# Strassen's scheme for six of eleven tile pairs of the down products in a one-core decoder layer

## The reference, cut to what matters

```python
def swiglu(x, wg, wu, wd):
    return (jax.nn.silu(x @ wg) * (x @ wu)) @ wd      # 1024 -> 2816 -> 1024

def trunk_layer(...):
    x = layer_norm(DN_ALPHA * x + 0.5 * swiglu(x, wg_l[0], wu_l[0], wd_l[0]), g_l[0], b_l[0])
    y, ks, vs, cs = token_mixer(x, attend, conv_prev, w_in_l, conv_w_l, w_out_l)
    x = layer_norm(DN_ALPHA * x + y, g_l[1], b_l[1])
    x = layer_norm(DN_ALPHA * x + 0.5 * swiglu(x, wg_l[1], wu_l[1], wd_l[1]), g_l[2], b_l[2])
```

## Time and profile before

| | |
|---|---|
| median of 3 runs | 1014.18 us |
| time of the profiled execution | 1012.97 us |
| its span | 1011.2 us |
| PE busy | 981.6 us, 97% of the span |
| DVE busy | 666.4 us, 66% |
| ACT busy | 468.9 us, 46% |
| POOL busy | 118.5 us, 12% |
| mean granted TensorE clock | 0.994 |

### The profile page before, as it was taken

One profiled execution on the slowest core, in us unless ns is written; L12 is line 12 of the kernel. 1 busy time (PEld: TensorE's weight loads), 2 busy tenths in 40 slices (PEclk: granted clock), 3 DMA queues, 4 the chain that ended last, 5 costly groups with the idle time before them and its releaser, 6 DMA issues.

```text
span 1011.2 us, 18213 instructions
## 1 busy us (share of the span) xinstructions
PE 981.6 (97%) x7538; PEld 961.5 (95%) x7538; DVE 666.4 (66%) x964; ACT 468.9 (46%) x780; POOL 118.5 (12%) x120
## 2 busy tenths in 40 slices
PE   7999999999999999999999998999999999999994
PEld 7999999999999999999898998999999999999994
DVE  5797642567776468736667678998534577774466
ACT  4465421255555235555555456664422345553230
POOL 2100000101100000107242012010000000000004
PEclk9999999999999999999999999999999999999998
DMA  9546356445435234362022457063453444445403
GB/s 262 128 114 168 105 114 154 96 121 118 106 95 188 94 116 84 102 193 83 13 74 71 139 155 187 21 168 95 135 147 64 104 105 112 126 140 172 136 1 89
DMA packets 142474, 118.68 MB, mean 117 GB/s; under 512 B 13778, under 2 KB 140470, under 8 KB 142376
## 3 DMA queue, kind: packets, MB, share of 16 engines
q1 hardware_dynamic: 130368, 105.46, 34.8%
q0 software_dynamic: 10880, 10.49, 7.5%
q10 hardware_dynamic: 1144, 1.57, 1.3%
HBM read 113.56 MB, written 4.95 MB: 117 GB/s over the span
## 4 chain that ended last, share of the span: by engine, by line
PE 88%; DVE 6%; ACT 3%; issue 1%; DMA 1%; DVEq 0%; SPq 0%; POOL 0%; ACTq 0%
PE banks L1058 41%; PE banks L1071 24%; PE banks L881 17%; PE banks L1243 2%; DVE w_lo L1821 1%; ACT w_hi L1367 1%; ACT x_hi L1549 1%; DMA w_raw<-in_ffn_w_gate 1%; PE banks L1289 1%; PE banks L1287 1%; DVE rstd L2077 1%; PE banks L935 1%; DVE x_res L2084 1%; DVE x_res L2064 0%; DVE w_lo L1849 0%
## 5 line engine op out<-in xcount | busy, mean ns | idle before, releaser
L1071 PE MATMUL banks<-h_hi,w_hi 128*128 128x280 f32 (+1 forms) x480 | 139.1, 290 | 0.0
L1071 PE MATMUL banks<-h_hi,w_lo 128*128 128x280 f32 (+1 forms) x480 | 139.0, 290 | 0.0
L1071 PE MATMUL banks<-h_lo,w_hi 128*128 128x280 f32 (+1 forms) x480 | 138.8, 289 | 0.0
L881 PE MATMUL banks<-x_hi,w_hi 128*128 128x280 f32 (+1 forms) x416 | 126.2, 303 | 3.9 <-DVE w_lo L1821 1.7
L881 PE MATMUL banks<-x_hi,w_lo 128*128 128x280 f32 (+1 forms) x416 | 120.9, 291 | 0.0
L881 PE MATMUL banks<-x_lo,w_hi 128*128 128x280 f32 (+1 forms) x416 | 120.8, 290 | 0.0
L1058 PE MATMUL banks<-x_hi,w_hi 128*128 128x280 f32 (+1 forms) x400 | 115.8, 290 | 0.4 <-DVE x_res L2034 0.4
L1821 DVE TENSOR_TENSOR w_lo<-w_raw,w_hi 128x1024 fp32r<-128x1024 f32 (+1 forms) x66 | 77.9, 1183 | 57.6 <-ACT w_hi L1367 57.1
L1058 PE MATMUL banks<-x_hi,w_lo 128*128 128x280 f32 (+1 forms) x400 | 115.8, 290 | 0.0
L1058 PE MATMUL banks<-x_lo,w_hi 128*128 128x280 f32 (+1 forms) x400 | 115.6, 289 | 0.0
L1058 PE MATMUL banks<-t_hi,w_hi 128*128 128x280 f32 x336 | 98.4, 293 | 1.9 <-ACT ln_sum L1469 1.9
(11 more groups left out here) (238 smaller groups left out, 2670.5 us busy)
## 6 DMA issues: line engine op xcount, KB each, us to landing
w_raw<-in_ffn_w_down SPq DMA_DIRECT2D x30, 512.0 KB, 4.1
more_raw<-in_ffn_w_down SPq DMA_DIRECT2D x28, 512.0 KB, 3.6
w_raw<-in_ffn_w_gate SPq DMA_DIRECT2D x24, 512.0 KB, 4.1
w_raw<-in_ffn_w_up SPq DMA_DIRECT2D x24, 512.0 KB, 5.0
more_raw<-in_ffn_w_gate SPq DMA_DIRECT2D x20, 512.0 KB, 4.3
more_raw<-in_ffn_w_up SPq DMA_DIRECT2D x20, 512.0 KB, 5.3
w_raw<-in_w_in SPq DMA_DIRECT2D x14, 512.0 KB, 4.6
more_raw<-in_ffn_w_up POOLq DMA_DIRECT2D x20, 256.0 KB, 4.6
```

The lines of the kernel that those rows point to most:

```text
L881: mm = nc.tensor.matmul(out[:, 0:n], w[:, t, :], x(k), start=(k == ends[0] and w is hi and x is rhs_hi), stop=(k == ends[1] and w is lo))
L1071: mm = nc.tensor.matmul(out, w[:, k - k0, c * P:(c + 1) * P], h[:, k, cols(half, f)], start=(k == 0 and w is hi and h is h_hi), stop=(ku = ...
```

## The change

Of the eleven pairs of hidden tiles, pairs 0 to 5 are now multiplied with the down weights by Strassen's scheme; the first pair (made plainly, added in a step of its own) and pairs 6 to 9 stay plain. The groups run in the order of `GROUPS`: pairs 0, 1, 2, then two *quads* (a quad is a Strassen group that makes four output tiles for all tokens) over pairs 0 and 1, then pairs 3, 4, 5, two quads over pairs 2 to 5, then pairs 6 to 9, then the plain down product of the last eight hidden tiles. In the text below the quads are Q00, Q01 (chunk 0) and Q10, Q11 (chunk 1).

A unit of Q00 and Q01 has 4 tiles (128x512), a step there 12 matmuls; they have an eighth step for the first pair (48 matmuls in four parts, the last waits for `z_evacuated`). A unit of Q10 and Q11 has 8 tiles, a step 24 matmuls. All results of quads are added into `x_res` by DVE straight from PSUM (`quad_add`, two output tiles at a time), eight adds in a quad of chunk 0, seven in one of chunk 1.

The hidden values of pairs 0 to 5 are kept as seven blocks each: three of Strassen's seven operands are hidden values themselves, four (the T blocks) are differences that DVE makes (`hidden_combinations`, three instructions), ACT rounds (`hidden_combo_hi`) and DVE splits (`hidden_combo_lo`). Part of that is done in the steps of the next group. The buffers for it take room: the raw ring has 6 slots instead of 8. S1 of a quad is made by adding transfers too. `bias_residual` of the first half (`f` = 0) moves from the down product to the mixer's first steps. The diff, cut to its core:

```diff
-RAWS = 8
+RAWS = 6
-A_PAIRS = 4
-K_UNITS = (((0, 4), (4, 8), (8, A_TILES)), ((0, 4), (4, 8), (8, H_TILES)))
+S_PAIRS = ((0, 1), (2, 3, 4, 5))
+C_TILES = 2 * (N_PAIRS - C_FIRST)
+K_UNITS = ((0, 4), (4, C_TILES))
+GROUPS = (("pair", 0), ("pair", 1), ("pair", 2), ("quad", 0, 0), ("quad", 0, 1), ("pair", 3), ("pair", 4), ("pair", 5),
+          ("quad", 1, 0), ("quad", 1, 1), ("pair", 6), ("pair", 7), ("pair", 8), ("pair", 9))
...
 def plan_loads():
-        if unit[0] != "st":
+        if unit[0] not in ("st", "sd") or unit[0] == "sd" and unit[4] == 7:
             keys.append((n, ""))
-        elif unit[3] == 0:
+        elif unit[-1] == 0:
             keys += [(n, b) for b in ("11", "12", "21", "22")]
...
-            r = (4, 5, 6, 7, 2, 3, 0, 1)[(i - end_fixed) % RAWS]
+            r = (4, 5, 2, 3, 0, 1)[(i - end_fixed) % RAWS]
...
+            def quad(f, chunk, qd):
+                js = S_PAIRS[chunk]
...
+                for b in ("11", "12", "21", "22"):
+                    key = (quad_unit(f, chunk, qd), b)
...
+                    raw_free(key)
+                    sp.dma_start(raw(key, QT)[:, 0:len(js), :],
...
+                if chunk == 0:
+                    key = (quad_unit(f, chunk, qd) + 7, "")
+                    raw_free(key)
...
+            def group_free(f, G, s):
+                if s == 0:
...
+                        pe.wait_ge(h0_done, G - 1)
+                elif s == 1:
+                    if g:
+                        pe.wait_ge(c11_done, G)
+                elif s == 2:
+                    pe.wait_ge(p1_copied, G + 1)
+                elif s == 3:
+                    if g:
+                        pe.wait_ge(c12_done, G)
+                elif s == 4:
+                    pe.wait_ge(u2_copied, G + 1)
+                elif s == 5:
+                    pe.wait_ge(p5_copied, G + 1)
+                else:
+                    pe.wait_ge(c22_done, G + 1)
...
+            def quad_step(f, chunk, qd, s):
+                pe.wait_ge(lo_ready, n + 1)
+                group_free(f, G, s)
+                if qd == 0 and s in (2, 3, 4, 6):
+                    pe.wait_ge(h_combo_ready, q)
+                for k, j in enumerate(js):
+                    if qd == 0 and s in (0, 1):
+                        pe.wait_ge(h0_ready, N_PAIRS * f + j + 1)
...
+            def quad_first(f, qd):
+                for i, (out, c, half) in enumerate(((z, 0, 0), (y, 0, 1), (x, 2, 0), (z, 2, 1))):
+                    if i == 3:
+                        pe.wait_ge(z_evacuated, 2 * f + qd + 1)
...
+            def down_start(f):
+                for ku in range(KU):
+                    pe.wait_ge(lo_ready, n0 + ku + 1)
+                    q = N_PAIRS * f + C_FIRST + K_UNITS[ku][1] // 2
+                    pe.wait_ge(h0_ready, q)
...
```

ACT's steps of a pair:

```diff
+            def pair_step(f, j, s):
...
+                elif s == 6:
+                    first_half_hi(f, j)
+                    if j == N_SP - 1:
+                        hidden_combo_hi(f, j)
+                next_hi(following(n))
+                if s == 1:
+                    silu_first(f, j)
+                elif s == 2 and before is not None:
+                    hidden_combo_hi(f, before)
```

DVE's steps of a pair and of a quad, and POOL's adding transfers:

```diff
             def pair_step(f, j, s):
...
+                elif s == 3 and before is not None:
+                    hidden_combo_lo(f, before)
                 elif s == 4:
                     add_c22(f, j)
                 elif s == 5:
                     add_c12(f, j)
                 elif s == 6:
                     gate_first(f, j)
+                    if j == N_SP - 1:
+                        hidden_combinations(f, j, 0)
+                        first_half_lo(f, j)
+                        hidden_combinations(f, j, 1)
+                        hidden_combinations(f, j, 2)
                 next_lo(following(n))
-                if s == 5:
+                if s < 2 and before is not None:
+                    hidden_combinations(f, before, 1 + s)
+                elif s == 5:
                     gate_second(f, j)
                 elif s == 6:
                     second_half_lo(f, j)
-                    first_half_lo(f, j)
+                    if j == N_SP - 1:
+                        hidden_combo_lo(f, j)
+                    else:
+                        first_half_lo(f, j)
+                        if j < N_SP:
+                            hidden_combinations(f, j, 0)
...
+            def quad_step(f, chunk, qd, s):
+                if s == 3 and pair_before is not None:
+                    hidden_combo_lo(f, pair_before)
...
+                if s == 0:
+                    quad_add(f, chunk, qd, (0, 0), x, p1_copied, first=not alone)
+                elif s == 1 and alone:
+                    quad_add(f, chunk, qd, (0, 0), z, c11_done)
+                elif s == 2:
+                    quad_add(f, chunk, qd, (0, 1), x, u2_copied, first=not alone)
+                elif s == 3:
+                    quad_add(f, chunk, qd, (1, 1), y, p5_copied, first=not alone)
+                elif s == 4:
+                    quad_add(f, chunk, qd, (1, 1), x, c22_done)
...
+                if s < 7:
+                    next_lo(following(n))
+                    if s < 2 and pair_before is not None:
+                        hidden_combinations(f, pair_before, 1 + s)
+                    return
+                dve.wait_ge(steps_done, DONE["first", f, qd, 0])
+                quad_add(f, chunk, qd, (0, 0), z, z_evacuated)
...
+            def second_row_sum(f, key):
+                pool.wait_ge(weights_in[RAW[n0, "21"]], ARRIVED[n0, "21"])
+                m = tiles_of(n0) // 4
+                for k in range(0, 2 * m, m):
+                    nc.gpsimd.dma_start(raw((n0, "21"), QT)[:, k:k + m, :], w[:, k:k + m, :], accum_op=ALU.add
+                                        ).then_inc(s1_summed[G % 2], 16)
```

More of the change, by code:

```diff
@@ L84, in plan_units @@
         out += [("gu", f, u) for u in range(4)]
[L85 to L90, removed]
+        for key in GROUPS:
+            if key[0] == "pair":
+                out += [("st", f, key[1], s) for s in range(7)]
+            else:
+                out += [("sd", f, key[1], key[2], s) for s in range(7 if key[1] else 8)]
+        out += [("dn", f, cp, ku, half) for half in range(2) for cp in range(C_PAIRS) for ku in range(KU)]
         if f == 0:
@@ L162, in plan_steps @@
             t = t0 + 8
-        elif unit[0] == "st":
+        elif unit[0] == "sd" and unit[4] == 7:
+            for i in range(4):
+                done["first", unit[1], unit[3], i] = t + i + 1
+            t += 4
+            free[n] = t
+        elif unit[0] in ("st", "sd"):
             t += 1
@@ L166, in plan_steps @@
         elif unit[0] == "dn":
-            _, f, chunk, cp, ku, half = unit
-            if half is None:
-                if ku < KU - 1:
+            _, f, cp, ku, half = unit
+            if cp == 0 and half == 0:
+                if ku == KU - 1:
                     t += 1
-                else:
[L172 to L175, removed]
+                    done[f, 0, 0] = t
+                    t += 1
+                    done[f, 1, 0] = t
+                else:
+                    t += 1
             else:
@@ new lines, in quad_first @@
+            def quad_first(f, qd):
+                G, n, off = group(f, "quad", 0, qd), quad_unit(f, 0, qd) + 7, N_META * f
+                x, y, z = group_banks(G)
+                hi, lo = split_hi(n, 2), split_lo(n, 2)
+                pe.wait_ge(lo_ready, n + 1)
+                pe.wait_ge(h_ready, 4 * f + 4)
+                for i, (out, c, half) in enumerate(((z, 0, 0), (y, 0, 1), (x, 2, 0), (z, 2, 1))):
+                    if i == 3:
+                        pe.wait_ge(z_evacuated, 2 * f + qd + 1)
+                    c0 = off if half == 0 else 0
+                    for ab in range(2):
+                        for k in range(2):
+                            for w, h in ((hi, g_hi), (hi, g_lo), (lo, g_hi)):
+                                mm = nc.tensor.matmul(out[:, ab, c0:HALF], w[:, k, (c + ab) * P:(c + ab + 1) * P],
+                                                      h[:, k, half * HALF + c0:(half + 1) * HALF],
+                                                      start=(i == 3 and k == 0 and w is hi and h is g_hi),
+                                                      stop=(k == 1 and w is lo), skip_group_check=i < 3)
+                    mm.then_inc(steps_done, 1)
@@ new lines, in quad_add @@
+            def quad_add(f, chunk, qd, block, bank, done, first=False):
+                r, half = block
+                c, off = 4 * qd + 2 * r, N_META * f if half == 0 else 0
+                x = x_res[:, c:c + 2, half * HALF + off:(half + 1) * HALF]
+                if first:
+                    op = nc.vector.scalar_tensor_tensor(x, x, ALPHA, bank[:, :, off:HALF], ALU.mult, ALU.add)
+                else:
+                    op = nc.vector.tensor_tensor(x, x, bank[:, :, off:HALF], ALU.add)
+                op.then_inc(done, 1)
```

(2 more changed lines are left out.)

613 lines of the change are left out of this document (344 added, 269 removed).

## The result

The changed kernel takes **1144.59 us** (median of 4 runs, 1138.98 to 1147.78) against 1013.67 us beside it (4 runs): a ratio of **1.1285, 95% interval 1.1239 to 1.1331**. Forecast were 1059 us, 1035 to 1083. The direction was right; the loss is 131 us and not 45.

The account below looks back on a forecast made before the run. The prediction took PE's dense matmuls as the bound, with late sums making PE wait: 1012.97 - 17.4 (matmuls removed) + 64.2 (waits, 32.1 a block) + 0.5 (POOL) - 1.5 (mixer wait) = 1059 us, range 1035 to 1083.

Parts of the forecast that it names:

- the ring's chain: From the lo of unit 4 to S1: block "21" and two adding transfers take 13.7 us (12.7 to 15.2), 11.5 available.
- the clock: Rival, chance 0.10: four long PE waits each start a slow stretch of matmuls, 4 x 1.7 us, giving 1066 us.
- First adding transfer 4 us after the lo of unit 4: Expected profile sign: POOL's first adding transfer of a group starts that long after DVE's lo; block alone about 4.1 us.
- the last landing of 4.6 us: End of the chain before S1: the second adding transfer takes 4.6 us from start to landing.
- the middle term: Inside the chain before S1: the second adding transfer starts 5.0 us after the first.
- since '21' now mostly travels alone: Reason given for taking 13.7 us for the chain instead of the 15.2 us measured with other loads beside it.
- S1 of the two chunk-0 quads is cheap ... I take nothing: Q00 and Q01: smaller block and half-size adding transfers; at worst 1 us of PE in Q00, counted as nothing.
- The row I leaned on: Profile before, 620 to 634: PE waited 3.8 us in all and the granted clock stayed 1.00.
- The matmuls removed: Both down products: 72 fewer matmuls per block save 9.3 us and 8.1 us, together 17.4 us on PE's path.
- DVE's order at the seams: DVE's added queue work makes PE wait 3.3 us in Q00, 0.5 in Q01, 4.7 in Q10, 1.7 at down start.
- sums in time: Rival, chance 0.09: adding transfers do not wait for each other, chain 9.9 us, DVE's order remains; 1018 us.
- Faster, PE stays the bound: Rival, chance 0.06: S1 within 11.5 us, DVE within 0.7 us of PE, only removed matmuls count; 994 us.

Follow-up runs that it names:

- e1: The kernel before with six raw slots instead of eight, nothing else changed: 1091.92 us, ratio 1.0749.
- e10: The kernel before with six raw slots and block "21" sent for first in all pairs but pair 0: 1013.39 us, ratio 0.9993.
- e3: The changed kernel with 1536 instead of 1024 bytes a partition for the descriptors of POOL's transfers: 1102.72 us, ratio 1.0872.
- e5: The changed kernel with block "21" first, and the bias table sent in four pieces at the starts of four groups: 1049.17 us, ratio 1.0344.
- e9: e8 with PE's order in Q10 changed too and more of DVE's queue reordered: 1022.05 us, ratio 1.0079.
- e2: The changed kernel with block "21" sent for first in every group but pair 0: 1061.29 us, ratio 1.0450.
- e8: e6 with DVE's queue reordered at five places at the seams: 1027.73 us, ratio 1.0138.
- e6: e5 with 1536 bytes a partition for the descriptors of POOL's transfers: 1044.85 us, ratio 1.0304.

## Why the forecast was right in kind and wrong in size

The sum by its own places, PE's waits in both blocks:

| place | forecast, us | after, first + second block |
|---|---|---|
| pairs 0 to 2 | 13.0 | 10.3 + 9.5 |
| Q00 | 6.6 | 3.0 + 3.1 |
| Q00's `quad_first`, for Q01's sums | 0 | 22.1 + 0 |
| Q01, for pair 3's sums, and its small waits | 14.4 | 7.8 + 9.1 |
| pairs 4 to 8, Q11 and after | 17.4 | 15.0 + 17.1 |
| Q10 | 9.4 | 2.6 + 2.9 |
| start of the down product | 3.4 | 3.2 + 3.4 |
| all | 64.2 | 109.1 |

Three terms of the sum failed, and one came out too small: the ring's chain (22 us dearer in the pairs), the bias table (22 us, taken as nothing), the clock (31 us, left out of the sum) and the saving (some 10 us short).

- **The ring, right as a mechanism.** "First adding transfer 4 us after the lo of unit 4" came as 4.05, the last landing of 4.6 us as 4.5. **The step that failed is the middle term:** 5.0 us from the first to the second adding transfer were 6.4 in the median of the pair groups and 8.05 in the chain shown, the worst; that chain is 16.6 us for 13.7, above the upper bound of 15.2. The reason I gave for the low value, "since '21' now mostly travels alone", was wrong: "21" did (3.7 us), the adding transfer behind it did not. Within 3 us of its start "22" and two blocks of the next group, 512 KB each, are sent for; it takes 7.7 us to land, and the second, with hardly a load beside it, 4.5. This made the steady pairs 15 us and the first ones 7 us dearer. e1 and e10 show the ring is the cause and the order of the loads its cure, e3 what the missing room adds.
- **"S1 of the two chunk-0 quads is cheap ... I take nothing":** right in the second block, wrong by 22 us in the first. The transfer of the bias table, which the change moves from behind pair 3 to the start of Q00, was missing from the sum. In the kernel before it holds loads up too (13 to 26 us to landing for the five 512 KB blocks sent for from 136 to 160 us), but it goes out at the start of the plain down product, and PE waits for none of them. No run takes the table alone out of the kernel after; the second block, which has none, and e5 stand for that.
- **The clock, a rival at 0.10, was the case.** Its price of 1.7 us for one slow stretch was right (31 us for 18); the number was not, 18 for 4. The row I leaned on, 3.8 us of waits between 620 and 634 at clock 1.00, holds one wait of 3.05 us (until 624.0). At the same place the kernel after waits 3.04 us (until 699.3), and there the clock falls; it also falls at a wait of 1.74 us (until 273.8). So a wait's length alone does not tell, and one row without a fall was no ground to leave the clock out of the sum. The rule of the Trainium skill (TensorE: Matmul & The Clock Gate, section "Why this matters for your kernels"), that idle gaps between bursts of matmuls send the clock back, agrees with this trace: 0.54 after a gap of 4.54 us, and 1.00 after one of 2.19 us.
- **The matmuls removed:** 17.4 us were 9.4 in e9, the version with least waits. The dense pace was right for the quads; what the step left out is that matmuls beside a wait or a stall do not keep it, and the change makes more of these.
- **DVE's order at the seams, right without the lateness:** e2's second block has 3.2 us in Q00 (forecast 3.3), 2.9 in Q10 (4.7 less 2.15), 1.3 in Q01 (0.5). The down start had 3.4 us for 1.7: DVE's lo of a down block and second-half split stand ahead of the split that PE needs, and putting that first took the wait to 0.7 us (e8). Pair 1 had 4.1 us where the rival "sums in time" gave 1.
- **"Sums in time", 1018 us,** is about what e2 to e8 tried to reach: with the ring's cost gone and the table split, 1044.85 us. Its 23.6 us at the seams are 34 us of waits in e6, counted as in the table; the clock's rest and the 10 us on the matmuls come on top. *Faster, PE stays the bound* is out: even e9 keeps 16 us more idle time than the kernel before.

From 1059 us to the 1144 measured: 45 us of waits (22 of them the table), 31 us of clock and some 10 us of matmuls that did not get saved.

## What to carry to other kernels

The smaller ring here did not cost by its size but by who stands where in it: put first the load that has the longest work behind it, and give each load its slot's release and its due time before you count slots. Price a wait of some us on the dense engine twice: for itself, and, where the granted clock falls, for the matmuls at half pace behind it. List every DMA in a moved or newly crowded stretch, those of other engines' queues too, and ask what is sent for behind it.

## What the chip showed beyond what I expected

- POOL's two adding transfers of 256 KB excluded each other for want of descriptor room: with 1024 bytes a partition the second starts 4.8 to 8.05 us after the first, with 1536 it starts 0.7 us after it, and each takes 8.3 to 8.5 us beside the other. Sizes between were not tried. The two of 128 KB in a chunk-0 quad start 0.6 us apart with 1024 bytes already.
- One transfer of 1.47 MB from ACT's queue made 512 KB loads land after 22.9 to 24.5 us, against 3.7 to 4.9 us for those sent for just before and just after, while all DMA together moved some 50 GB/s in a third of that time; e5 shows what one piece at this place costs, not why it is so slow.
- The clock's part was nearly a third of the waits' (31 to 106 us). In e10, with no wait from 194 to 325 us, the granted clock there is 1.00; in e1, the same matmuls with waits, it is 0.96.
